# Encoder trunk: the second attention in groups of 512 queries, the inverse sums multiplied in one step later, and the last norm's second half on token rows

## The reference

```python
for i in range(DEPTH):                      # 2 layers, S = 1024 tokens, D = 1024
    u = x * (1.0 + sc1) + sh1
    y = diff_attention(u, ...) if i == 0 else mla_attention(u, ...)
    x = _layer_norm(DEEPNORM_ALPHA * x + (1.0 + g1) * y, ln_g[i, 0], ln_b[i, 0])
    u = x * (1.0 + sc2) + sh2
    y = squared_relu_mlp(u, ffn_w1[i], ffn_w2[i])
    x = _layer_norm(DEEPNORM_ALPHA * x + (1.0 + g2) * y, ln_g[i, 1], ln_b[i, 1])
# mla_attention, 16 heads, for each block of 128 queries against all keys up to its own end:
#   s = (q_nope k_nope^T + q_rope k_rope^T) * scale, masked;  p = softmax(s);  o = p v  (64 values a head)
#   then the heads' outputs, 1024 wide, times w_o
```

## Time and profile before

| what | us |
|---|---|
| runs of the kernel before | 2934.16, 2934.26, 2934.52 (median 2934.26) |
| the profiled execution | 2934.04 |
| its span | 2932.4 |
| second attention | about 1565 to 2083 of the span |
| from the last product's end to the span's end | 2893.1 to 2932.4 |

### The profile page before, as it was taken

The page is one execution under the profiler, slowest core; times in us unless marked ns, Lnnn a source line. Parts: engine busy times, 40 slices in busy tenths (PEclk is TensorE's granted clock), DMA queues, the critical chain, the costliest instruction groups (busy, mean ns, idle before and its releaser), DMA issues.

```text
span 2932.4 us, 37871 instructions
## 1 busy us (share of the span) xinstructions
PE 2668.8 (91%) x12716; PEld 2189.5 (75%) x12716; DVE 1654.3 (56%) x2830; ACT 1163.9 (40%) x2093; POOL 328.5 (11%) x346
## 2 busy tenths in 40 slices
PE   3899989879999999999997888888699999999996
PEld 2677777767788888887776777777577888888884
DVE  4477777747653443543757777777376233232356
ACT  2365666634512213123454665566245122130323
POOL 0000000001110000160324222222010000000000
PEclk8999999989999999999999999999899999999997
DMA  8233333363342331412331111111633111111122
GB/s 316 74 90 103 111 93 104 92 224 90 101 136 85 90 118 50 137 57 68 117 95 23 28 29 30 29 27 43 220 90 87 57 50 50 43 50 50 50 80 79
DMA packets 333440, 254.17 MB, mean 87 GB/s; under 512 B 41192, under 2 KB 303639, under 8 KB 332319
## 3 DMA queue, kind: packets, MB, share of 16 engines
q1 hardware_dynamic: 317518, 194.21, 22.9%
q0 software_dynamic: 14736, 50.34, 5.6%
q10 hardware_dynamic: 1088, 8.39, 0.7%
HBM read 215.12 MB, written 33.59 MB: 85 GB/s over the span
## 4 chain that ended last, share of the span: by engine, by line
PE 63%; DVE 13%; ACT 11%; issue 9%; DMA 3%; DVEq 0%; ACTq 0%; SPq 0%; POOL 0%
PE PA L1693 31%; PE SC L1693 26%; DVE H L1219 2%; DVE soft L1608 2%; ACT H L749 2%; DVE W L1128 1%; ACT X L1054 1%; ACT X L765 1%; PE TB L1700 1%; DMA x_rows<-in_x 1%; ACT W L702 1%; PE SC L1801 1%; PE VB L1785 1%; DVE X L1630 1%; DMA attention_out<-ostage 1%
## 5 line engine op out<-in xcount | busy, mean ns | idle before, releaser
L1693 PE MATMUL PA<-U,W 128*128 128x512 f32 x3840 | 950.3, 402 | 81.5 <-DVE W L1128 44.4
L1693 PEld LDWEIGHTS PA<-U,W 128*128 128x128 f32 x3840 | 726.0, 191 | 251.9 <-issue 57.2
L702 ACT ACTIVATE W<-raw 128x1024 fp32r<-128x1024 f32 (+2 forms) x262 | 260.1, 994 | 816.4 <-PE PA L1693 390.1
L1693 PE MATMUL SC<-U,W 128*128 128x512 f32 x2064 | 481.1, 391 | 4.0 <-DVE W L1128 3.7
L1693 PEld LDWEIGHTS SC<-U,W 128*128 128x128 f32 x2064 | 387.2, 188 | 90.2 <-DVE W L1128 4.9
L1128 DVE TENSOR_TENSOR W<-raw,W 128x1024 fp32r<-128x1024 f32 (+2 forms) x262 | 315.4, 1204 | 99.6 <-ACT W L702 98.3
L1693 PE MATMUL PA<-H,W 128*128 128x512 f32 x1536 | 358.6, 392 | 3.2 <-DVE W L1128 3.2
L1693 PE MATMUL SC<-H,W 128*128 128x512 f32 x1536 | 354.4, 390 | 0.0
L1693 PEld LDWEIGHTS PA<-H,W 128*128 128x128 f32 x1536 | 288.5, 189 | 64.3 <-DVE W L1128 3.6
L1693 PEld LDWEIGHTS SC<-H,W 128*128 128x128 f32 x1536 | 288.4, 188 | 60.7 <-issue 1.0
L1392 DVE SCALAR_TENSOR_TENSOR X<-PA,aff,X 128x512 f32 (+1 forms) x80 | 60.0, 750 | 211.5 <-PE PA L1693 211.5
(11 more groups left out here) (221 smaller groups left out, 3037.3 us busy)
## 6 DMA issues: line engine op xcount, KB each, us to landing
raw<-in_ffn_w SPq DMA_DIRECT2D x160, 512.0 KB, 4.0
ada<-in_ada_w POOLq DMA_DIRECT2D x80, 512.0 KB, 4.6
U<-attention_out SPq DMA_DIRECT2D x4, 3584.0 KB, 17.5
raw<-in_da_w_qkv SPq DMA_DIRECT2D x24, 512.0 KB, 5.2
ada_first<-in_ada_w ACTq DMA_DIRECT2D x4, 2048.0 KB, 18.1
H<-H SPq DMA_DIRECT2D x32, 256.0 KB, 5.3
attention_out<-ostage SPq DMA_DIRECT2D x32, 256.0 KB, 2.9
raw<-in_da_w_o SPq DMA_DIRECT2D x16, 512.0 KB, 4.0
```

What stands on the lines that cost most here:

```text
L702: nc.scalar.activation(W[:, slot, 0, 0:kt * P], raw[:, slot, 0:kt * P], ACT.Copy).then_inc(w_hi, 1)
L1693: ins = mm(bank, W[:, slot, a, kt * P:(kt + 1) * P], moving(b, kt)[:, cols], start=kt == first and (a, b) == SPLIT[0], stop=kt == last and ...
```

## The change

**Output in groups of 512 queries.** `values1` runs twice a head, at s = 4 and at s = 0 of the next head, into the whole of VB: 24 matmuls a head of up to 512 columns (the same 9216 columns in all). The inverse sums are transposed four at a time into a bank of the probabilities' turn order (`inverses1`), which ACT copies to SBUF (`copy_l`). DVE then does one product for each group (`scale_out`, 128 x 512), and the rest goes a step at a time: ACT lower half (`out_bottom1`), POOL sum (`out_sum1`), ACT high part one step later (`out_hi1`), POOL low part (`out_lo1`). The two reciprocals a head take four columns each instead of eight of one. The low parts of the next head's weights move from DVE to POOL (`split_lo1`), and the 512-column split is made a head earlier, at s = 6. The stores become two a head, 256 KB each, and `load_o` of tiles 0 to 6 now stands behind the second store of head 14.

**Last norm, second half.** Each tile of the second half is transposed to token rows in the middle of the next half product (`row_turn`, four transposes, seven times there and once at the end), copied by ACT (`row_copy`), and its row sums taken by DVE. After the last one the mean, variance and affine are done on rows, 128 tokens x 1024 at a time, with the gain and bias loaded to all partitions, and four stores of 512 KB.

```diff
+        ostage1, osum, obot = tmp[0:VD, 0:2, :], tmp[0:VD, 2, :], tmp[0:VD, 3, :]
+        linv, omul = ostage[:, :, :].rearrange("p a n -> p (a n)"), acc[:, :]
...
+                if not is_first(h):
+                    store_o1(h - 1, 1)
                 if final:
                     sp.wait_ge(HS[1]["pj_ready"], 4 * HEADS1)
-                    sp.wait_ge(HS[1]["o_stored"], 16 * 4 * (HEADS1 - 2))
                     load_o(1, 0, KT - 1)
-                for pair in range(4):
-                    store_o(1, h, pair, VD)
-            with sp.Fori(0, HEADS1 // 2 - 1) as i:
+                store_o1(h, 0)
+            def store_o1(h, g):
...
+            def out_sum1(h, g):
+                pool.wait_ge(HS[1]["o_sq"], 2 * h + g + 1)
+                nc.gpsimd.tensor_tensor(osum, omul[0:VD, :], obot, ALU.add).then_inc(HS[1]["o_sum"], 1)
+            def out_lo1(h, g):
+                pool.wait_ge(HS[1]["o_hi"], 2 * h + g + 1)
+                nc.gpsimd.tensor_tensor(ostage1[:, 1, :].bitcast(F32R), osum, ostage1[:, 0, :], ALU.subtract)\
+                    .then_inc(HS[1]["o_lo"], 1)
+            def split_lo1(g0, hi, kt):
+                slot = g0 % 2
+                pool.wait_ge(w_hi, g0 + 2 * hi + 1)
+                nc.gpsimd.tensor_tensor(W[:, slot, 1, 0:kt * P], raw[:, slot, 0:kt * P],
+                                        W[:, slot, 0, 0:kt * P].bitcast(F32), ALU.subtract).then_inc(w_lo, 1)
+            def heads1(h0, i, last=False):
+                h, p = h0 + 2 * i, h0 % 2
+                proj = not (last and h0 % 2)
+                g0 = G_HEADS1 + 2 * (h0 + 1)
+                own.body(h + 1, 2 * NH)
+                if is_first(h):
+                    split_lo1(g0, 2 * i, QT)
+                if proj:
+                    split_lo1(g0 + 1, 2 * i, KVT)
+                if not is_first(h):
+                    out_sum1(h - 1, 1)
+                if proj:
+                    rope_q(1 - p, h + 1, 0)
+                if not is_first(h):
+                    out_lo1(h - 1, 1)
+                out_sum1(h, 0)
+                if proj:
+                    rope_q(1 - p, h + 1, 1)
+                    own.end_body()
+                out_lo1(h, 0)
+                if not last:
+                    split_lo1(g0 + 2, 2 * i, QT)
...
+            def row_copy(t):
+                act.wait_ge(row_t, t + 1)
+                nc.scalar.activation(rows_y[:, :, t * P:(t + 1) * P],
+                                     row_bank(t)[:, :].rearrange("p (q d) -> p q d", d=P), ACT.Copy).then_inc(row_y, 1)
...
+            def copy_l(h, g, bank):
+                act.wait_ge(a1["o_inv"], 2 * h + g + 1)
+                if not (is_first(h) and g == 0):
+                    act.wait_ge(a1["o_fin"], 2 * h + g)
+                nc.scalar.activation(linv, bank[:, :], ACT.Copy).then_inc(a1["r_ready"], 1)
+            def out_bottom1(h, g):
+                act.wait_ge(a1["o_fin"], 2 * h + g + 1)
+                nc.scalar.activation(obot, omul[VD:P, :], ACT.Copy).then_inc(a1["o_sq"], 1)
+            def out_hi1(h, g):
+                act.wait_ge(a1["o_sum"], 2 * h + g + 1)
+                if not (is_first(h) and g == 0):
+                    act.wait_ge(a1["o_stored"], 16 * (2 * h + g))
+                nc.scalar.activation(ostage1[:, 0, :].bitcast(F32R), osum, ACT.Copy).then_inc(a1["o_hi"], 1)
...
-                    if s == 1 and not is_first(h):
-                        out_bottom(h - 1, 3)
-                        out_hi(a1, h - 1, 3, VD, osum[0:VD, :])
-                    if s in (3, 5, 7):
-                        out_bottom(h, (s - 3) // 2)
-                        out_hi(a1, h, (s - 3) // 2, VD, osum[0:VD, :])
+                    if s == 2 and not is_first(h):
+                        out_bottom1(h - 1, 1)
+                    if s == 3 and not is_first(h):
+                        out_hi1(h - 1, 1)
+                    if s == 6:
+                        out_bottom1(h, 0)
+                    if s == 7:
+                        out_hi1(h, 0)
+                    if is_first(h) and s == 0:
+                        split_uq(g0, 2 * i, h + 1, a1["pj_ready"], 4 * h + 3)
                     if proj and s == 0:
-                        split_uq(g0, 2 * i, h + 1, a1["pj_ready"], 4 * h + 3)
-                    if proj and s == 2:
                         split_hi(g0 + 1, 2 * i, KVT, a1["pj_ready"], 4 * h + 4)
+                    if not last and s == 6:
+                        split_uq(g0 + 2, 2 * i, h + 2, a1["pj_ready"], 4 * h + 7)
                     if not proj and s == 0:
                         split_hi(G_WO1, 0, KT, a1["pj_ready"], 4 * HEADS1)
+                    if s == 0 and not is_first(h):
+                        copy_l(h - 1, 1, t1_bank(I_LATE, p))
+                    if s == 4:
+                        copy_l(h, 0, t1_bank(I_EARLY, p))
...
+            row_copy(KT - 1)
+            act.wait_ge(row_m, 1)
+            for q in range(4):
+                nc.scalar.activation(ada[:, q % 2, :, :].rearrange("p b n -> p (b n)"), rows_y[:, q, :], ACT.Square,
+                                     bias=row_mean[:, q:q + 1], accum_out=row_sq[:, q:q + 1]).then_inc(row_q, 1)
+                act.wait_ge(row_q, q + 1)
+                nc.scalar.activation(row_inv1[:, q:q + 1], row_sq[:, q:q + 1], ACT.Ln, scale=1.0 / D, bias=eps_ln)\
+                    .then_inc(row_l, 1)
+                act.wait_ge(row_l, q + 1)
+                nc.scalar.activation(row_inv1[:, q:q + 1], row_inv1[:, q:q + 1], ACT.Exp, scale=-0.5).then_inc(row_r, 1)
...
-            def sum_out(h, pair):
-                dve.wait_ge(a1["o_sq"], 4 * h + pair + 1)
-                dve.wait_ge(a1["o_lo"], 4 * h + pair)
-                nc.vector.tensor_tensor(osum[0:VD, :], VB[0:VD, 0:PAIR], obot[0:VD, :], ALU.add).then_inc(a1["o_sum"], 1)
-                dve.wait_ge(a1["o_sum"], 4 * h + pair + 1)
-                nc.vector.tensor_tensor(osum[0:VD, :], osum[0:VD, :], VB[0:VD, PAIR:2 * PAIR], ALU.mult)\
-                    .then_inc(a1["o_fin"], 1)
-                out_lo(a1, h, pair, VD, osum[0:VD, :])
...
+            def scale_out(h, g):
+                dve.wait_ge(a1["o_ready"], 2 * h + g + 1)
+                dve.wait_ge(a1["r_ready"], 2 * h + g + 1)
+                if not (is_first(h) and g == 0):
+                    dve.wait_ge(a1["o_sum"], 2 * h + g)
+                nc.vector.tensor_tensor(omul, VB[:, :], linv, ALU.mult).then_inc(a1["o_fin"], 1)
...
-            ln_add(E_MLP1 + MLP_PRODUCTS - 1, KT - 1, 1)
-            for step in range(KT):
-                ln_dve(3, 1, step)
+            row_sum1(KT - 2)
+            row_sum1(KT - 1)
+            dve.wait_ge(row_s, KT)
+            own(nc.vector.tensor_reduce(row_mean, row_sums.rearrange("p t q -> p q t"), mybir.AxisListType.X, ALU.add))
+            nc.vector.tensor_scalar(row_mean, row_mean, -1.0 / D, None, ALU.mult).then_inc(row_m, 1)
+            dve.wait_ge(row_m, 1)
+            dve.wait_ge(row_in, 32)
+            def row_center(q):
+                nc.vector.scalar_tensor_tensor(rows_out[:, q, :], rows_y[:, q, :], row_mean[:, q:q + 1], rows_g,
+                                               ALU.add, ALU.mult).then_inc(row_c, 1)
+            def row_scale(q):
+                dve.wait_ge(row_r, q + 1)
+                dve.wait_ge(row_c, q + 1)
+                nc.vector.scalar_tensor_tensor(rows_out[:, q, :], rows_out[:, q, :], row_inv1[:, q:q + 1], rows_b,
+                                               ALU.mult, ALU.add).then_inc(row_e, 1)
+            row_center(0)
+            for q in range(1, 4):
+                row_center(q)
+                row_scale(q - 1)
+            row_scale(3)
...
+            def row_turn(t):
+                pe.wait_ge(d_evac, E_MLP1 + MLP_PRODUCTS - KT + t + 1)
+                if t >= 2:
+                    pe.wait_ge(row_y, t - 1)
+                for q in range(4):
+                    ins = transpose_to(row_bank(t)[:, q * P:(q + 1) * P], X[:, t, HALF + q * P:HALF + (q + 1) * P])
+                ins.then_inc(row_t, 1)
...
+            def inverses1(h, g, free, bank):
+                pe.wait_ge(a1["l_inv"], 2 * h + g + 1)
+                pe.wait_ge(a1["t_evac"], free)
+                for k in range(4):
+                    ins = nc.tensor.transpose(bank[:, k * P:(k + 1) * P], row_inv(4 * g + k).to_broadcast([P, P]), ident)
+                ins.then_inc(a1["o_inv"], 1)
+            def values1(h, g):
+                last = 4 * g + 3
+                pe.wait_ge(a1["o_fin"], 2 * h + g)
                 for j in range(last + 1):
-                    c0 = 0 if j < last else P
+                    if j % 4 == 0:
+                        pe.wait_ge(a1["t_evac"], evacuated(h, turn_of(last, j // 4)))
+                    c0 = max(0, j - 4 * g) * P
                     for b in (1, 0):
-                        ins = mm(VB[:, c0:PAIR], V1[:, j, :], at1(pair)[:, b, j, c0:PAIR], start=j == 0 and b == 1,
```

(59 more changed lines are left out.)

168 lines of the change are left out of this document (97 added, 71 removed).

## The result

| | us |
|---|---|
| kernel before, median of 4 runs | 2934.39 (2934.16 to 2935.0) |
| changed kernel, median of 4 runs | 2896.6 (2895.17 to 2902.49) |
| ratio, 95% interval | 0.9875, 0.9858 to 0.9892 |
| the profiled execution after, and its span | 2895.53, 2893.8 |

The change saves 38 us; the forecast was 50. The sign held and the number missed by 12.6. The range held by 1.4 us only, and one of the four runs, 2902.49, lies above it. First PE in order of time, one head from piece 3 to piece 3 (the earlier trace rows before). The rows of the output's matmuls are left out.

A forecast was written before the change was run, and what follows sets the result against it. PE was nearest to full, but its waits, chiefly for DVE, counted as well. 2934.04 - 25.5 (heads) - 7 (attention's end) - 17.9 (last norm) = 2883.6, stated as 2884 us; range 2868 to 2898.

The forecast's parts named there:

- A: Head from piece 3 to step 2's transposes, 9.31 us: grows by 0.9 with the output group of 6656 columns.
- B: Head from step 2's transposes to piece 1, 5.97 us: falls by 1.3, the wait for the weight split going.
- C: Head from piece 1 to step 6's transposes, 10.58 us: falls by 0.25, with less idling for low parts.
- D: Head from step 6's transposes to the next piece 3, 5.77 us: falls by 1.05, ACT no longer being late.
- Fifteen heads pass before the last one begins: -25.5 us: Attention heads: each 1.7 us shorter, 29.9 instead of 31.6, over the fifteen before the last; bounds -15 and -86.
- The prediction's own sign of being wrong: Attention head length: forecast 29.9 us, called wrong if a head is above 30.5 or below 29.
- The attention's end: From the last head's start to its last store: 40.5 us instead of 47.5, so -7 us; bounds 0 and -11.
- The last norm: From the last product's end to the span's end: 21.4 us instead of 39.3, so -17.9; bounds -15 and -19.
- 1, waits that come back through the hand-overs: Attention heads: ACT or PE waits for POOL's sum instead; heads gain only 0.6, 2900 us; chance 0.17.
- 2, PE as the bound: Attention heads: DVE's chains shrink to PE's work, 2.5 us more for most heads, 2846 us; chance 0.16.
- 3, POOL too slow: Weight splits on POOL: at 2.6 us per instruction a head lasts 35, 2959 us, slower; chance 0.04.
- 4: Last norm or attention's end: their change does little, 10 us less gain, 2894 us; no separate chance, inside the range.

The follow-up runs named there:

- kv_dve: Changed kernel with only the 256-column low part of the next head's weights back on VectorE, behind `lo_piece` at s = 2; 2921.16 us.
- fill_all: Changed kernel with twelve extra PE transposes ahead of each piece 1 and eight ahead of each piece 3; 2883.89 us.
- norm_only: Kernel before the change with only the last norm's second half on token rows, nothing of the attention; 2917.0 us.
- pool_3x: Changed kernel with POOL's 512-column low part made three times, each behind the one before; 2920.34 us.
- end_load: Changed kernel with the load of output tiles 0 to 6 issued ahead of the second store of head 14; 2900.44 us.
- fill_p3: Changed kernel with eight extra 128 x 128 PE transposes before each piece 3, into idle bank VB; 2889.0 us.

## Why the prediction was right in its mechanism and 12 us short

**A head.** The four stretches of the head of 1745.95, with the forecast's change and the measured one: A 10.27 (+0.9; +0.96), B 4.54 (-1.3; -1.43), C 10.22 (-0.25; -0.36), D 4.82 (-1.05; -0.95). Together -1.7 forecast, -1.78 measured. Piece 1 was released by `lo_piece` 4.54 behind step 2's transposes (4.7 forecast); PE waits 0.26 ahead of the inverse sums (0.4); POOL's 128 x 512 takes 1.28 (1.38). `kv_dve` shows that B is the offload's: the 256-column split alone is worth 1.15 a head, nearly its whole length of 1.22, and that length is long because POOL works beside it.

**The step that failed** is the multiplication: "Fifteen heads pass before the last one begins: -25.5 us". It took a head without a fall for the mean one. The kernel before bore that out, since there the two differ by 0.04. In the changed kernel six of the seven falls lie behind piece 3, in stretch A, which PE sets, with the idling of step 7 (0.80) and of piece 3 (1.13) ahead of them. The seventh lies behind piece 1's 1.57. Seven falls of 1.4 us make 30.57 out of 29.86 for 14 heads. In place of -25.5, head 15 begins 15.8 earlier (2040.22 - 2024.41). The prediction's own sign of being wrong, a head above 30.5, is met by this mean and not by the head that it had drawn, 29.85.

**The account**, profiled execution against the sum (2895.53 to 2883.6, 11.9 short): the 14 heads 8.4 (30.57 against 31.67 - 1.7); from piece 1 of head 14 to the third slab 76.3 measured against 80.5 - 1.7 - 7 = 71.8, 4.5; the last norm 0.7 better; the attention's start 0.4 better. With the waits filled, 14 heads take 29.86 and that end 73.5 to 74.2. That `fill_all`'s 2883.9 is the forecast's number is in part luck: its 14 heads are 1.5 us shorter than forecast in all, they begin 1.2 earlier (1577.77), the last norm is 0.6 better, and the end, 74.1, is 2.3 worse.

**The attention's end.** For the whole stretch, head 14 included, the forecast was -7 - 1.7 = -8.7, and -4.2 was measured. From head 15's start (2024.41) the tiles were called at 14.1 (13.6 forecast), the store behind landed at 37.0 (35.9), the last store at 42.0 (40.5), the third slab's product began at 58.5 (55.7): 2.8 late in small sizes along the right chain. The other 1.7 lie in head 14, which has a fall at 2021 and is as long as before the change. What bounds this end is not the third slab's call but, beside it, the residual's load with DVE's order behind it; the forecast didn't see that, and it cost nothing, because the two come together.

**The last norm.** Forecast -17.9. Measured 21.5 less behind the last product and 2.9 more ahead of it (third slab to last product, 793.1 against 790.2), so -18.6; `norm_only` gives -18.5 by itself.

**Rivals.** 1, waits that come back through the hand-overs: ACT's 2.7 us waits are gone, and no head without a fall has lost its gain; its time (2900) was near the measured one for another reason. 2, PE as the bound: no, B's and D's chains still release pieces 1 and 3. 3, POOL too slow: the mechanism is real (`pool_3x`), but from 1.2 us more work on, not at its measured size. 4: no. The Trainium skill's advice to keep two-input work on VectorE ("GPSIMD Engine Reference", Engine selection), weighed there, would have cost more than the attention's gain here: `kv_dve`, with the 256-column split alone on VectorE, is 24.6 us above the changed kernel, and that gain is about 19. What counted was which engine the chain to piece 1 ran through.

Open: the cause of the 2.2 us in `end_load`; why the same two waits ahead of piece 3 bring a fall in six of the changed kernel's 14 heads and none in the others; why two of 14 heads still had a fall behind piece 1 in `fill_p3` while most did not; and what the 512-column split on VectorE at s = 0 would cost in the changed kernel.
